# One stage in place of two at the end of each RWKV head pair: gate and memory products issued inside the scan

## The reference, cut to what matters

```python
def step(s, inp):
    r_t, w_t, k_t, v_t, aa_t, bb_t = inp
    sa = jnp.einsum('dbhij,dbhj->dbhi', s, aa_t)
    s = s * w_t[..., None, :] + sa[..., :, None] * bb_t[..., None, :] + v_t[..., :, None] * k_t[..., None, :]
    y_t = jnp.einsum('dbhij,dbhj->dbhi', s, r_t)
    return s, y_t

def rwkv_output(y, r, k_d, v, g, r_k, gn_g, gn_b):
    mean = jnp.mean(y, -1, keepdims=True)
    var = jnp.mean(jnp.square(y - mean), -1, keepdims=True)
    yn = (y - mean) * lax.rsqrt(var + GN_EPS) * heads(gn_g) + heads(gn_b)
    bonus = jnp.sum(r[:, :, None] * k_d * r_k, -1, keepdims=True) * v[:, :, None]
    return jnp.sum((yn + bonus).reshape(b_, t, N_DIR, RWKV_WIDTH) * g, axis=2)

mod = (jax.nn.silu(c) @ w_ada[l] + b_ada[l])[:, None, :]   # six vectors of 1024
```

## Time and profile before

| | |
|---|---|
| median of 3 runs | 3538.15 us (3538.09 to 3543.82) |
| profiled execution, its time | 3534.93 us |
| its span from first to last instruction | 3533.1 us |
| mean granted TensorE clock | 0.940 |
| PE busy | 3189.2 us, 90% of the span |
| DVE, ACT, POOL busy | 1393.7, 998.8, 151.0 us |
| scan and output of the four pairs | begin at 346.2, 469.7, 594.2 and 718.6 us |

### The profile page before, as it was taken

One profiled execution on the slowest core, in us unless ns is written; L12 is line 12 of the kernel. 1 busy time (PEld: TensorE's weight loads), 2 busy tenths in 40 slices (PEclk: granted clock), 3 DMA queues, 4 the chain that ended last, 5 costly groups with the idle time before them and its releaser, 6 DMA issues. The chain is left out here.

```text
span 3533.1 us, 64359 instructions
## 1 busy us (share of the span) xinstructions
PE 3189.2 (90%) x25961; PEld 2065.9 (58%) x25962; DVE 1393.7 (39%) x2384; ACT 998.8 (28%) x1792; POOL 151.0 (4%) x210
## 2 busy tenths in 40 slices
PE   4998888975999999999999979977899899878998
PEld 3887768764333333333333358765688688655786
DVE  5545655565111111111111167345533364546333
ACT  3343432421111111111111123344422223435221
POOL 0000000012000000000000200000000000000000
PEclk8999988986999999999999889987999999979999
DMA  6730232054999999989989733130132232310331
GB/s 228 245 122 27 81 102 96 9 190 177 393 374 409 410 368 361 409 314 407 409 310 409 306 99 94 45 62 25 49 96 96 70 85 84 49 37 1 108 96 60
DMA packets 273089, 645.82 MB, mean 183 GB/s; under 512 B 36890, under 2 KB 97050, under 8 KB 270978
## 3 DMA queue, kind: packets, MB, share of 16 engines
q1 hardware_dynamic: 255746, 605.14, 47.4%
q0 software_dynamic: 6224, 21.24, 1.6%
q10 hardware_dynamic: 10928, 16.79, 1.4%
HBM read 599.83 MB, written 43.27 MB: 182 GB/s over the span
## 5 line engine op out<-in xcount | busy, mean ns | idle before, releaser
L1745 PE MATMUL ps<-raw,ex_xT 128*64 128x512 f32 x3072 | 677.9, 593 | 4.8 <-DMA raw<-in_w_dram 4.8
L1745 PEld LDWEIGHTS ps<-raw,ex_xT 128*64 128x64 f32 x3072 | 218.2, 137 | 419.3 <-issue 407.3
L1844 DVE TENSOR_SCALAR ex_gl<-ps 128x256 f32<-128x256 f32 x96 | 40.8, 425 | 948.6 <-PE ps L1745 948.6
L1745 PE MATMUL ps<-raw,ex_aT 128*64 128x512 f32 x1536 | 349.1, 596 | 3.0 <-DMA raw<-in_w_dram 3.0
L1745 PEld LDWEIGHTS ps<-raw,ex_aT 128*64 128x64 f32 x1536 | 105.5, 137 | 214.4 <-issue 206.8
L2005 PE MATMUL ps<-zhi,hl 128*128 128x512 f32 (+1 forms) x448 | 169.7, 379 | 0.0
L2003 PE MATMUL ps<-zhi,hh 128*128 128x512 f32 (+1 forms) x448 | 169.1, 378 | 0.0
L2004 PE MATMUL ps<-zlo,hh 128*128 128x512 f32 (+1 forms) x448 | 168.6, 376 | 0.0
L2550 PE MATMUL ps<-uu_hi,hh 128*128 128x512 f32 x384 | 151.4, 394 | 10.6 <-DVE uu_lo L2662 10.6
L2552 PE MATMUL ps<-uu_hi,hl 128*128 128x512 f32 x384 | 152.8, 398 | 0.0
L2551 PE MATMUL ps<-uu_lo,hh 128*128 128x512 f32 x384 | 152.3, 397 | 0.0
(11 more groups left out here) (584 smaller groups left out, 5975.4 us busy)
## 6 DMA issues: line engine op xcount, KB each, us to landing
raw<-in_w_dram SPq DMA_DIRECT2D x384, 1024.0 KB, 18.9
oT<-in_w_in_dram SPq DMA_DIRECT2D x64, 512.0 KB, 3.6
u_raw<-in_w_in_dram SPq DMA_DIRECT2D x24, 1024.0 KB, 5.3
expert_out<-xn SPq DMA_DIRECT2D x4, 4096.0 KB, 16.7
expert_out<-ex_yrow ACTq DMA_DIRECT2D x98, 128.0 KB, 5.6
late_ada<-in_w_ada_dram SPq DMA_DIRECT2D x12, 1024.0 KB
early_w<-in_w_in_dram SPq DMA_DIRECT2D x10, 1024.0 KB, 6.7
kv_memT<-memory_turned SPq DMA_DIRECT2D x8, 1024.0 KB, 5.8
```

The costliest lines, as they stand in the source:

```text
L1745: mm = pe.matmul(o, x, M["raw"][:, (slot + LATE_SLOTS) % RING, k, h * 512:(h + 1) * 512], start=(s >= 8 and kk == 0), stop=(kk == 7))
```

## The change

The two stages become one, `rwkv_close`, so that the engines no longer meet between them, and the work is spread anew. TensorE: after each of the scan's first four steps two gate products, after each of the other seven two products of the memory head; ahead of the first of these it waits for `kv0_in`. The last two memory products follow on the products of `seen`, and then the modulation. The bias of the modulation is no longer a product: GpSimd adds it to the finished row. The scan's products write one PSUM bank for each direction and no longer two. ScalarE copies the gates to SBUF (`W["gate"]`), and takes the square root between the copies of the memory head and those of the modulation. GpSimd multiplies `base` by the gate, the gate by the norm's gain, and sums `base` over the two directions, so that VectorE, after the norm, multiplies once, adds the two directions and adds `base`: three instructions in place of four. SyncE issues the `kv1` loads once `seen` and the last states are there.

```diff
-def rwkv_scan(nc, A, ps, T, W, c, memt, kv0_in, ada_in):
+def rwkv_close(nc, A, ps, T, W, c, memt, kvrows, kv0_in, kv1_in, ada_in, mods, mods_kept):
...
+    GATES, SEEN, HEADS, MODS, SUMS, TURNED = 2, 4, 6, 0, 2, 7
...
         @block.sync
         def _(sp):
             load_head(sp, A, W["memT0"], W["wkv0"], 0, c, memt, kv0_in)
             load_modulation(sp, A, W, c, ada_in)
+            if c < 3:
+                for d in range(2):
+                    sp.wait_ge(state[d], NCH - 1)
+                sp.wait_ge(seen, 1)
+                load_head(sp, A, W["memT1"], W["wkv1"], 1, c + 1, memt, kv1_in)
+            sp.wait_ge(kv_out, 2)
+            keep_head(sp, kvrows, W["kvout0"], 0, c, kv_kept)
+            sp.wait_ge(mod_out, 1)
+            sp.dma_start(mods[:, c * 1024:(c + 1) * 1024], W["modrow"][:, :]).then_inc(mods_kept, 16)
+            sp.wait_ge(kv_kept, 32)
 
         @block.gpsimd
...
+            pool.wait_ge(gate_kept, 1)
+            pool.tensor_tensor(W["base"][:, :], W["base"][:, :], W["gate"][:, :], ALU.mult).then_inc(shaped, 1)
+            pool.wait_ge(shaped, 1)
+            gate = W["gate"][:, :].rearrange("p (g s) -> p g s", s=P)
+            pool.tensor_tensor(gate, gate, bc(T["gng"][:, c * P:(c + 1) * P], 1, 8), ALU.mult).then_inc(shaped, 1)
+            both = W["base"][:, :].rearrange("p (t d s) -> p t d s", d=2, s=P)
+            pool.tensor_tensor(both[:, :, 0, :], both[:, :, 0, :], both[:, :, 1, :], ALU.add).then_inc(shaped, 1)
+            pool.wait_ge(ada_in, 80 * (c + 1))
+            pool.wait_ge(mod_row, 2)
+            pool.tensor_tensor(W["modrow"][:, :], W["modrow"][:, :], W["adab"][:, :], ALU.add).then_inc(mod_out, 1)
...
         @block.tensor
         def _(pe):
+            def gate(i):
+                d, tt = i // TT, i % TT
+                return pe.matmul(ps[:, GATES + tt // 2, (tt % 2 * 2 + d) * P:(tt % 2 * 2 + d + 1) * P],
+                                 T["mT"][:, 14 + d, tt * P:(tt + 1) * P], T["g2"][:, d, c * P:(c + 1) * P], start=True, stop=True)
+
+            def head(i):
+                m, k = i // KD, i % KD
+                return pe.matmul(ps[:, HEADS, m * 256:(m + 1) * 256], W["memT0"][:, k, m * P:(m + 1) * P],
+                                 W["wkv0"][:, k, :, :].rearrange("p s d -> p (s d)"), start=(k == 0), stop=(k == KD - 1))
+
+            heads = 0
             pe.wait_ge(zeroed, 1)
             for n in range(NCH - 1):
                 for d in range(2):
                     if n:
                         pe.wait_ge(state[d], n)
                     for hs in halves:
-                        last = pe.matmul(ps[hs, 2 * d + n % 2, 0:HS], W["gt"][hs, d, order[d][n], :], W["states"][hs, d, n, :], start=True, stop=True)
+                        last = pe.matmul(ps[hs, d, (n % 2) * HS:(n % 2) * HS + HS], W["gt"][hs, d, order[d][n], :], W["states"][hs, d, n, :], start=True, stop=True)
                     last.then_inc(moved[d], 1)
+                if n < TT:
+                    gate(2 * n)
+                    last = gate(2 * n + 1)
+                    if n == TT - 1:
+                        last.then_inc(gates, 1)
+                        pe.wait_ge(kv0_in, 48 * (c + 1))
+                else:
+                    for i in range(2):
+                        last = head(heads + i)
+                    heads += 2
...
             last.then_inc(seen, 1)
+            for i in range(heads, 2 * KD):
+                last = head(i)
+            last.then_inc(kv_prod, 1)
+            pe.wait_ge(ada_in, 80 * (c + 1))
...
+            pe.wait_ge(gate_kept, 1)
+            for q in range(2):
+                pe.wait_ge(part_out, q + 1)
+                pe.matmul(ps[:, SUMS + q, :], S("row0"), W["part"][:, q, :], start=True, stop=True).then_inc(ada_sum, 1)
+            pe.wait_ge(rw, 1)
+            for tt in range(TT):
+                last = pe.transpose(ps[:, TURNED, tt * P:(tt + 1) * P], rows_done[:, tt, :], S("ident"))
+            last.then_inc(turned, 1)
+
+        @block.scalar
+        def _(act):
+            act.wait_ge(gates, 1)
+            act.activation(W["gate"][:, :], ps[:, GATES:GATES + 2, :].rearrange("p a b -> p (a b)"), ACT.Copy).then_inc(gate_kept, 1)
+            act.wait_ge(kv_prod, 1)
...
+            act.wait_ge(var_in, 1)
+            act.activation(W["var"][:, :], W["var"][:, :], ACT.Sqrt).then_inc(root, 1)
+            for q in range(2):
+                act.wait_ge(ada_prod, q + 1)
+                act.activation(W["part"][:, q, :], ps[:, MODS + q, :], ACT.Copy).then_inc(part_out, 1)
...
+            act.wait_ge(turned, 1)
+            act.activation(T["mixT"][:, c, :], ps[:, TURNED, :], ACT.Copy).then_inc(mixed, 1)
...
         @block.vector
...
             dve.wait_ge(seen, 1)
             for h in range(2):
...
-                dve.tensor_tensor(y, y, ps[:, 4 + h, :].rearrange("p (g s) -> p g s", s=HS), ALU.add).then_inc(added, 1)
-            dve.wait_ge(added, 2)
...
+                done(dve.tensor_tensor(mine, mine, ps[:, SEEN + h, :].rearrange("p (g s) -> p g s", s=HS), ALU.add))
...
             done(dve.tensor_tensor(y, y, bc(W["var"][:, :], 2, HS), ALU.mult))
+            dve.wait_ge(shaped, 3)
...
-            done(dve.tensor_tensor(y3, y3, bc(T["gng"][:, bass.ts(c, P)], 1, 8), ALU.mult))
-            done(dve.tensor_tensor(y3, y3, W["base"][:, :].rearrange("p (g s) -> p g s", s=P), ALU.add))
-            dve.wait_ge(gates, 1)
-            done(dve.tensor_tensor(y3, y3, ps[:, 0:2, :].rearrange("p a (g s) -> p (a g) s", s=P), ALU.mult))
-            dve.tensor_tensor(W["rw"][:, :, :], W["yr"][:, :, 0, :], W["yr"][:, :, 1, :], ALU.add).then_inc(rw, 1)
+            done(dve.tensor_tensor(y3, y3, W["gate"][:, :].rearrange("p (g s) -> p g s", s=P), ALU.mult))
+            done(dve.tensor_tensor(rows_done, W["yr"][:, :, 0, :], W["yr"][:, :, 1, :], ALU.add))
+            dve.tensor_tensor(rows_done, rows_done, W["base"][:, :].rearrange("p (t d s) -> p t d s", d=2, s=P)[:, :, 0, :], ALU.add).then_inc(rw, 1)
```

More of the change, by code:

```diff
@@ L1110, in _ @@
                         for h, hs in enumerate(halves):
-                            last = pe.matmul(ps[cs, 4 + h, (2 * t2 + d) * HS:(2 * t2 + d + 1) * HS], W["qt"][hs, d, t2, cs], W["states"][hs, d, n, :],
+                            last = pe.matmul(ps[cs, SEEN + h, (2 * t2 + d) * HS:(2 * t2 + d + 1) * HS], W["qt"][hs, d, t2, cs], W["states"][hs, d, n, :],
                                              start=True, stop=True)
             last.then_inc(seen, 1)
+            for i in range(heads, 2 * KD):
+                last = head(i)
@@ new lines, in _ @@
+            last.then_inc(kv_prod, 1)
+            pe.wait_ge(ada_in, 80 * (c + 1))
+            for q in range(2):
+                for k in range(KD):
+                    j = k % 4
+                    last = pe.matmul(ps[32 * j:32 * j + 32, MODS + q, :], T["cpad"][:, k, :], W["ada"][2 * q + k // 4][:, k % 4, :], start=(k < 4), stop=(k >= 4))
+                last.then_inc(ada_prod, 1)
+            pe.wait_ge(gate_kept, 1)
+            for q in range(2):
+                pe.wait_ge(part_out, q + 1)
+                pe.matmul(ps[:, SUMS + q, :], S("row0"), W["part"][:, q, :], start=True, stop=True).then_inc(ada_sum, 1)
@@ L1115, in _ @@
         @block.vector
         def _(dve):
+            done = Chain(dve, dve_step)
             dve.memset(W["states"][:, :, 0, :], 0.0).then_inc(zeroed, 1)
@@ L1125, in _ @@
             for h in range(2):
-                y = W["yr"][:, :, :, h * HS:(h + 1) * HS].rearrange("p t d s -> p (t d) s")
-                dve.tensor_tensor(y, y, ps[:, 4 + h, :].rearrange("p (g s) -> p g s", s=HS), ALU.add).then_inc(added, 1)
-            dve.wait_ge(added, 2)
[L1131 to L1168, removed]
-                pe.matmul(ps[:, (3, 7)[q], :], T["onerow"][:, :], W["adab"][:, q * 512:(q + 1) * 512], start=False, stop=True).then_inc(ada_sum, 1)
-            pe.wait_ge(rw, 1)
-            for tt in range(TT):
-                last = pe.transpose(ps[:, 2, tt * P:(tt + 1) * P], W["rw"][:, tt, :], S("ident"))
-            last.then_inc(turned, 1)
-        @block.scalar
-        def _(act):
-            act.wait_ge(var_in, 1)
-            act.activation(W["var"][:, :], W["var"][:, :], ACT.Sqrt).then_inc(root, 1)
-            act.wait_ge(kv_prod, 1)
-            for m in range(2):
-                act.activation(W["kvout0"][:, m, :], ps[:, 4, m * 256:(m + 1) * 256], ACT.Copy, scale=T["memrs"][:, m:m + 1]).then_inc(kv_out, 1)
-            for q in range(2):
-                act.wait_ge(ada_prod, q + 1)
-                act.activation(W["part"][:, q, :], ps[:, 5 + q, :], ACT.Copy).then_inc(part_out, 1)
-            if c:
-                act.wait_ge(mods_kept, 16 * c)
-            for q in range(2):
-                act.wait_ge(ada_sum, q + 1)
-                act.activation(W["modrow"][:, q * 512:(q + 1) * 512], ps[0:1, (3, 7)[q], :], ACT.Copy, bias=1.0 if c == 2 else 0.0).then_inc(mod_out, 1)
-            act.wait_ge(turned, 1)
```

(5 more changed lines are left out.)

30 lines of the change are left out of this document (23 added, 7 removed).

## The result

The changed kernel takes 3557.94 us (median of 5 runs, 3554.14 to 3562.9) against 3538.15 (5 runs, 3537.48 to 3543.82): a ratio of 1.0058, 95% interval 1.0046 to 1.007. It is 19.8 us slower; forecast were 11, with a range of 3536 to 3563. Its profiled execution has a span of 3555.2 us and a mean granted clock of 0.938.

A forecast was written before the change was run, and what follows sets the result against it. The scan's chain, then TensorE in the tail, was taken as the bound. Four pairs lose 42.8 us before `seen` and save 31.6 behind it: +11.2 on 3534.93 gives 3546, plus 3.2 for the median, 3549 us; range 3536 to 3563.

The forecast's parts named there:

- my own band of +7 to +18: Whole kernel: the prediction's main case, 3545 to 3556 us, given a chance of 0.54.
- a clock low for longer: Scan: TensorE's clock stays low through all or part of the seven steps, +18 to +34 us, chance 0.11.
- The wait for `kv0_in`: After the fourth scan step: TensorE idles 4 to 5 us until the weights land, hiding the gates; landing time unchanged.
- The seven steps: Scan steps five to eleven: 1.32 us each at high clock, 2.39 low; TensorE becomes the scan's bound.
- The clock: TensorE in the scan: low at the landing, high 3.8 us later, so seven steps take 10.9 us, 42.8 us lost.
- A sign misstated: Expected in the changed profile: `seen` at 17 to 19 us from the stage's start, against 9.4 to 10.2 before.
- The tail: From `seen` to the stage's end: 13.5 us instead of 21.4, saving 7.9 a pair, 31.6 in all.
- Taken as nothing: Start of the next stages: more TensorE idle time and perhaps a low clock, 0 to 4 us in all, counted 0.
- Steps cheaper: Scan, rival 1: clock high or shape changes free, 3535 to 3545 us; chance 0.27 together with early weights.
- Clock low throughout: Scan, rival 2: low clock through all seven steps, 16.7 us a pair, 3572 us; whole or in part 0.11.
- Weights landed by the fourth step: Scan, rival 4: the wait doesn't show, some 2 us a pair off, +3; chance 0.27 together with cheaper steps.
- Shadow of the big products: Scan, rival 3: scan passes hide under memory products, 0.87 us a step, -8 us, 3530 us; chance 0.08.

The follow-up runs named there:

- like tiles: Changed kernel without the wait, products reading resident tiles, each beside steps five to eleven split into two of 64 x 64 x 256: 1.10 us a step, 3521.49 us once.
- The repeated changed kernel: The changed kernel, nothing altered, measured again on the chip of a follow-up run: 3551.8 us, ratio 1.0058 to the kernel before.
- the run with the later loads: Changed kernel with memory head after `seen`, one gate a step, bias on VectorE, next pair's memory-head loads held until modulation's weights land: ratio 0.9957.

## Why the prediction was right, and where its sizes were off

Direction and mechanism held, the size was 11.2 for 19.8. That is inside the range, but above my own band of +7 to +18, and in the one that I had given to a clock low for longer, at 0.11.

In the spans of the two profiled executions the difference is 22.1 us, 10.9 more than the sum: `seen` comes 6.2 us later than forecast over the four pairs, the tail gives back 0.6 more, and 5.3 lie outside the four stages.

*The wait for `kv0_in`.* Right: 3.4 to 5.5 us of idle TensorE before the fifth step in each pair, ended by `kv_w`, with the gates hidden under it. The landing moved a little, to a mean of 9.9 us from the stage's start where it had been 9.5; counted as unchanged, that is 1.3 us in all.

*The seven steps.* Right in kind, TensorE being the bound of the scan, and mis-sized: 1.44 us for 1.32 high, 2.62 for 2.39 low, 3.6 us in all. The two memory products with what I had put on top for the changes of shape came out as summed, 1.06 for 1.07 high (754.52 - 753.46) and 2.00 for 1.96 low (744.45 - 742.45). The mis-sized term is the scan's own passes: 0.38 for 0.25 high (753.46 - 753.08) and 0.62 for 0.43 low (742.45 - 741.83). With like tiles they take 0.23, so this too is the change of shape: 0.34 a step in all, where the earlier trace rows, which show only the way from full to smaller tiles, had given 0.19 for both ways.

*The clock.* Right that it is low at the landing in each pair; in the fourth by luck, as it had fallen before the wait. I took the rise 3.8 us after the landing; it came after 3.4, 3.9, 5.1 and 5.8, which is 1.3 us in all. From the landing to `seen` went 11.6 us in the first pair and 12.7 in the fourth, 12.2 in the mean, for 10.9. With the landing, the four pairs lose 49.0 us here and not 42.8.

*A sign misstated.* I had written that `seen` would begin 17 to 19 us from the stage's start. My own sum says 9.8 + 10.7 = 20.5; it began at 21.5 to 22.5.

*The tail.* 8.1 us saved a pair for 7.9 forecast, in part by luck: 0.8 of them are `seen`, which I had taken as unchanged and which ran at the high clock, and what is behind it saved 7.2. VectorE's 11.4 came out as said, GpSimd's bias row took 2.51 for 2.4 (2.33 in the first pair) and was the last work, the table load stayed hidden. Not foreseen: TensorE's idle time let the clock fall in the tail, so that the sums ran low (3.62 us for four in the first pair, 1.98 high).

*Taken as nothing.* The next stages' start, put at 0 to 4 us and counted 0, is 1.9 us between the pairs in this one profile. Behind the fourth pair 4.4 us more went, 1.9 of them in the stage that runs from 1244 to 1306 us behind it, 0.8 in each of two ahead of that, and the rest in small pieces. The repeated changed kernel has 0.6 less than before there, so I call none of it the change's; what it is stays open.

*The rivals.* Steps cheaper: no, dearer. Clock low throughout: no, for some 1.3 to 2.2 of the seven. Weights landed by the fourth step: no, TensorE waited for them in each pair. Shadow of the big products: the step would have had to be under 0.90 us; even with like tiles it is 1.10.

## What to carry to other kernels

Before work is moved forward onto an engine that others wait for, look up when its operands land, not when it now begins: a load that has been hidden for 7 us becomes the pace of the chain if its reader moves ahead of it. A chain of short steps has less room than its idle time says, as each filler brings its own length and its change of shape; fill with pieces smaller than the gap, or put the work behind the chain. And once a tail is short, the next transfer is its bound, so its landing belongs in the sum as well.

## What the runs showed that I had not expected

Two changes between 128 x 128 and 64 x 64 tiles cost 0.34 us in a step of 1.44, although the nearest row of before had shown 0.09 for one. That row was right for the way down: the last pass of a memory product before a scan product takes 0.31 us where it otherwise takes 0.22, as in the earlier trace rows. The way back up makes the other 0.25. `seen` took 1.1 us at the high clock where every row of before had 2.0, since it had always run low. And the end of a long transfer trails: in the run with the later loads the engines moved 383 GB/s to 363, then 74 and 29 GB/s for two more us, and only then was the wait released:

```profile
362.00:363.00 1.00, 0.17 (x1) 0.00 (x0) 0.68 (x3) 0.36 (x2) 0.00 (x0) 1.00 1.03 383
363.00:364.00 1.00, 0.00 (x0) 0.00 (x0) 0.97 (x2) 0.58 (x2) 0.00 (x0) 1.00 0.20 74
364.00:365.00 1.00, 0.00 (x0) 0.00 (x0) 0.97 (x2) 0.00 (x0) 0.00 (x0) 1.00 0.08 29
```
